# Norm scales from two token columns, spread to rows by transposes

## The reference

```
y = xf * lax.rsqrt(jnp.mean(xf * xf, axis=-1, keepdims=True) + NORM_EPS)
return (y * g.astype(jnp.float32)).astype(x.dtype)
```

```
for l in range(DEPTH):
    h = rms_norm(x, attn_norm_g[l])
    pa, pb, pc = split_sizes(h @ w_in[l], (A_PROJ, B_PROJ, C_PROJ))
    ...
    x = x + jnp.concatenate([ya, yb, yc], axis=-1) @ w_out[l]
    h = rms_norm(x, ffn_norm_g[l])
    x = x + (jax.nn.silu(h @ ffn_w_gate[l]) * (h @ ffn_w_up[l])) @ ffn_w_down[l]
return rms_norm(x, final_norm_g)
```

## Time and profile before

| | |
|---|---|
| Time, median of 3 runs | 939.88 us (939.52 to 940.46) |
| Span of the profiled execution | 938.7 us, with some 1.2 us around it to the median of the runs |
| Instructions in the span | 20423 |
| PE / PEld busy | 916.4 us (98%) / 869.5 us (93%) |
| DVE / ACT busy | 680.7 us (73%) / 555.8 us (59%) |
| Weight chunks on DVE (L277, 256 halves) | 306.0 us, 1224 ns each |
| Weight chunks on ACT (L271, 256 halves) | 259.4 us, 1054 ns each |
| HBM read | 147.26 MB, 158 GB/s over the span |

### The profile page before, as it was taken

How to read it: one execution, slowest core, us unless ns; L and a number is a source line. 1 busy time by engine, 2 the same in 40 slices (tenths; PEclk the granted TensorE clock), 3 DMA queues, 4 the chain that set the end, 5 groups by cost and what they waited for, 6 DMA issues and landing times.

```text
span 938.7 us, 20423 instructions
## 1 busy us (share of the span) xinstructions
PE 916.4 (98%) x8848; PEld 869.5 (93%) x8848; DVE 680.7 (73%) x972; ACT 555.8 (59%) x851; POOL 7.6 (1%) x12
## 2 busy tenths in 40 slices
PE   8899999999999999999999999999999999999996
PEld 7788799999999999878999999999989899989896
DVE  6899667866664589976777666448799679588675
ACT  6873566654443588355754544338587667585665
POOL 0010000000000001000000000000000000000000
PEclk9999999999999999999999999999999999999998
DMA  8342115665554544211466655554544335444231
GB/s 324 151 174 95 48 56 188 214 261 183 201 201 180 180 163 151 98 64 46 140 251 232 250 192 182 204 197 135 179 136 138 132 135 180 147 168 157 93 135 67
DMA packets 24169, 150.94 MB, mean 161 GB/s; under 512 B 2960, under 2 KB 3472, under 8 KB 7056
## 3 DMA queue, kind: packets, MB, share of 16 engines
q1 hardware_dynamic: 24080, 149.64, 44.7%
HBM read 147.26 MB, written 1.05 MB: 158 GB/s over the span
## 4 chain that ended last, share of the span: by engine, by line
PE 67%; DVE 20%; ACT 7%; issue 3%; SPq 1%; DMA 1%; DVEq 0%; ACTq 0%
PE bank L1914 9%; PE bank L1912 8%; PE bank L1913 8%; DVE w_lo L277 6%; PE bank L2145 4%; PE bank L1936 3%; PE bank L1934 3%; PE bank L1935 3%; PE bank L2146 3%; PE bank L2147 3%; ACT w_hi L271 2%; PE bank L1075 1%; PE bank L2177 1%; PE bank L589 1%; PE bank L1165 1%
## 5 line engine op out<-in xcount | busy, mean ns | idle before, releaser
L277 DVE TENSOR_TENSOR w_lo<-w_raw,w_hi 128x1024 fp32r<-128x1024 f32 x256 | 306.0, 1224 | 106.2 <-ACT w_hi L271 105.5
L271 ACT ACTIVATE w_hi<-w_raw 128x1024 fp32r<-128x1024 f32 x256 | 259.4, 1054 | 206.3 <-PE bank L1914 104.9
L1912 PE MATMUL bank<-act_hi,w_hi 128*128 128x256 f32 x704 | 194.5, 276 | 0.0
L1913 PE MATMUL bank<-act_lo,w_hi 128*128 128x256 f32 x704 | 194.3, 276 | 0.0
L1914 PE MATMUL bank<-act_hi,w_lo 128*128 128x256 f32 x704 | 194.3, 276 | 0.0
L1912 PEld LDWEIGHTS bank<-act_hi,w_hi 128*128 128x128 f32 x704 | 132.2, 188 | 0.1
L1913 PEld LDWEIGHTS bank<-act_lo,w_hi 128*128 128x128 f32 x704 | 132.2, 188 | 0.0
L1914 PEld LDWEIGHTS bank<-act_hi,w_lo 128*128 128x128 f32 x704 | 132.2, 188 | 0.0
L2145 PE MATMUL bank<-act_hi,w_hi 128*128 128x256 f32 x352 | 100.2, 285 | 0.3
L2147 PE MATMUL bank<-act_hi,w_lo 128*128 128x256 f32 x352 | 97.7, 278 | 0.0
L2146 PE MATMUL bank<-act_lo,w_hi 128*128 128x256 f32 x352 | 97.7, 278 | 0.0
(11 more groups left out here) (367 smaller groups left out, 1982.1 us busy)
## 6 DMA issues: line engine op xcount, KB each, us to landing
w_raw<-in_w_ffn SPq DMA_DIRECT2D x66, 1024.0 KB, 4.8
w_raw<-in_w_mix SPq DMA_DIRECT2D x62, 1024.0 KB, 4.9
small_w<-in_small SPq DMA_DIRECT2D x2, 1280.0 KB, 7.6
w_raw<-in_w_mix SPq DMA_DIRECT2D x8, 256.0 KB, 6.3
x_res<-in_x_channels SPq DMA_DIRECT2D x4, 256.0 KB, 6.1
probs<-in_w_mix SPq DMA_DIRECT2D x2, 512.0 KB, 7.5
probsT<-in_w_mix SPq DMA_DIRECT2D x1, 1024.0 KB, 10.1
mem<-in_mem_channels SPq DMA_DIRECT2D x1, 1024.0 KB, 7.2
```

The costliest lines, as they stand in the source:

```text
L271: self.nc.scalar.activation(hi, self.piece(self.raw_slot(g), p), ACT.Copy).then_inc(self.hi_ready, 1)
L277: self.nc.vector.tensor_tensor(lo, self.piece(self.raw_slot(g), p), hi.bitcast(fp32), ALU.subtract).then_inc(self.lo_ready, 1)
L1912: TE.matmul(o, hi[:, w], HI[:, k, :], start=(k == 0 and x == 0), stop=False)
L1913: TE.matmul(o, hi[:, w], LO[:, k, :], start=False, stop=False)
```

## The change

`spread` and `scaled_spread` lose the wide matmul and give only the two columns of sums. Root, reciprocal and, in `FoldedNorm`, the products are taken on two columns. A new step, `row_turn`, makes the row: two PE transposes of a column, broadcast over 128 columns, against the identity, put the scale of 256 tokens on every partition in PSUM, and ACT copies the row to `norm_rs` (`row`). The transposes stand inside a chunk: after its first quarter in the mixers (after the second in the stage of `FoldedNorm`, where a second pair turns the first scale), and after the fourth chunk of the feed-forward. The feed-forward's first `gate_sb` moves into the next chunk's halves on DVE, and in the mixers one or two halves of weights move ahead of the first `evacuate`. `settle` is gone. The memory's scale is turned in the same way, without the diagonal. The identity gets a transfer of its own (64 KB), ahead of the small weights.

```
+            last = self.nc.tensor.matmul(bank[:, T + t:T + t + 1], total[:, t * P:(t + 1) * P], ones[:, 0:1],
+                                         start=True, stop=True)
-        self.nc.tensor.matmul(bank[:, 0:T], ones, total, start=True, stop=True).then_inc(self.K.sem("rms_sum"), 1)
+        last.then_inc(self.K.sem("rms_sum"), 1)
...
-        self.nc.scalar.activation(self.K.RSALL[:, :], bank[:, 0:T + NT], ACT.Sqrt, scale=1.0 / D,
+        self.nc.scalar.activation(self.K.RS, bank[:, T:T + NT], ACT.Sqrt, scale=1.0 / D,
...
-        self.nc.vector.reciprocal(self.K.RSALL[:, :], self.K.RSALL[:, :]).then_inc(self.K.sem("rs"), 1)
-        self.wait_rs(dve)
+        self.nc.vector.reciprocal(self.K.RS, self.K.RS).then_inc(self.K.sem("rs"), 1)
+
+    def turn_columns(self, columns, bank):
+
+        for t in range(NT):
+            last = self.nc.tensor.transpose(bank[:, t * P:(t + 1) * P], columns[:, t:t + 1].to_broadcast([P, P]),
+                                            self.K.cst("ident"))
+        return last
+
+    def row_turn(self, pe, bank):
+        pe.wait_ge(self.K.sem("ident_in"), 16)
+        self.wait_rs(pe)
+        self.turn_columns(self.K.RS, bank).then_inc(self.K.sem("rms_sum"), 1)
+
+    def row(self, act, bank):
+        act.wait_ge(self.K.sem("rms_sum"), 2 * self.n + 2)
+        self.nc.scalar.activation(self.K.RSB, bank[:, 0:T], ACT.Copy).then_inc(self.K.sem("rms"), 1)
...
+    def wait_row(self, eng):
+        eng.wait_ge(self.K.sem("rms"), 2 * self.n + 2)
...
-        self.nc.vector.reciprocal(self.R1[:, :], self.K.RSALL[:, :]).then_inc(self.K.sem("first_rs"), 1)
+        self.nc.vector.reciprocal(self.R1[:, T:T + NT], self.K.RS).then_inc(self.K.sem("first_rs"), 1)
...
-            proj(pe, 2)
+            proj(pe, 2, (0,))
+            norm.row_turn(pe, banks[0])
+            proj(pe, 2, (1, 2, 3))
...
-            proj(pe, 1)
+            proj(pe, 1, (0,))
+            norm.row_turn(pe, banks[0])
+            proj(pe, 1, (1, 2, 3))
...
             if i == 2:
                 norm.spread(pe, banks[0])
-                settle(pe)
-        norm.wait_rs(pe)
+            elif i == 3:
+                norm.row_turn(pe, banks[0])
+        norm.wait_row(pe)
...
-        pe.wait_ge(*at("mem_rs_diag", NT))
-        TE.matmul(banks[0][:, 0:T], cst("ones"), DG, start=True,
-                  stop=True).then_inc(*up("inner_sums"))
+        pe.wait_ge(*at("mem_inverse", 1))
+        norm.turn_columns(MRC, banks[0]).then_inc(*up("inner_sums"))
...
-        proj(pe, 2)
+            proj(pe, 2, (0, 1))
+            norm.row_turn(pe, banks[0])
+            norm.first_row_turn(pe, banks[1])
+            proj(pe, 2, (2, 3))
```

More of the change, by code:

```diff
@@ L464, in scaled_spread @@
         for t in range(NT):
-            self.nc.tensor.matmul(bank[:, T + t:T + t + 1], total[:, t * P:(t + 1) * P], ones[:, 0:1], start=True, stop=True)
-        self.nc.tensor.matmul(bank[:, 0:T], ones, total, start=True, stop=True).then_inc(self.K.sem("scaled_rms_sum"), 1)
+            last = self.nc.tensor.matmul(bank[:, T + t:T + t + 1], total[:, t * P:(t + 1) * P], ones[:, 0:1],
+                                         start=True, stop=True)
+        last.then_inc(self.K.sem("scaled_rms_sum"), 1)
@@ L491, in second_inverse, with first_row_turn, first_row, wait_first_row @@
-        self.wait_rs(dve)
+        self.nc.vector.tensor_tensor(RS, RS, self.R1[:, T:T + NT], ALU.mult).then_inc(self.K.sem("rs"), 1)
+    def first_row_turn(self, pe, bank):
+        self.turn_columns(self.R1[:, T:T + NT], bank).then_inc(self.K.sem("scaled_rms_sum"), 1)
+    def first_row(self, act, bank):
+        act.wait_ge(self.K.sem("scaled_rms_sum"), 2)
+        self.nc.scalar.activation(self.R1[:, 0:T], bank[:, 0:T], ACT.Copy).then_inc(self.K.sem("second_rms"), 1)
+    def wait_first_row(self, eng):
+        eng.wait_ge(self.K.sem("second_rms"), 2)
@@ L1651, in _ @@
             st.split_hi(act, 2, 1)
+            norm.row(act, banks[0])
         else:
@@ L1757, in _ @@
             st.split_lo(dve, 2, 1)
+            norm.wait_row(dve)
             evacuate(dve, 0)
@@ L2008, in _ @@
             st.split_hi(act, i + 1, 0)
+            if i == 4:
+                norm.row(act, banks[0])
             st.split_hi(act, i + 1, 1)
@@ L2051, in _ @@
             st.split_lo(dve, i + 1, 0)
+            if i == 4:
+                norm.wait_row(dve)
+                gate_sb(dve, 0)
             st.split_lo(dve, i + 1, 1)
@@ L2331, in turn @@
         if i == 0:
-            norm.wait_rs(pe)
+            norm.wait_row(pe)
+        if i == 1 and layer == 0:
+            norm.wait_first_row(pe)
         TE.matmul(banks[i][:, :], cst("rotb"), PJ[:, S_MBQ + 2 * i:S_MBQ + 2 * i + 2, :],
@@ L2410, in mem_lo, with mem_inverse @@
                                    ALU.mult, ALU.subtract).then_inc(*up("mem_h_lo"))
-    def mem_diagonal(dve, ch):
+    def mem_inverse(dve, ch):
         dve.wait_ge(*at("inner_rms", 1))
[L2414 to L2417, removed]
+        ch(V.reciprocal(MRC[:, :], MRC[:, :]), "mem_inverse")
     def mem_row(dve, ch):
@@ L2442, in _ @@
         norm.spread(pe, banks[0])
-        proj(pe, 1)
         if layer == 0:
+            proj(pe, 1)
             norm.scaled_spread(pe, banks[1])
-        proj(pe, 2)
+            proj(pe, 2, (0, 1))
+            norm.row_turn(pe, banks[0])
+            norm.first_row_turn(pe, banks[1])
+            proj(pe, 2, (2, 3))
+        else:
+            proj(pe, 1, (0,))
+            norm.row_turn(pe, banks[0])
+            proj(pe, 1, (1, 2, 3))
+            proj(pe, 2)
         proj(pe, 3)
@@ L2520, in _ @@
             st.split_hi(act, 3, 1)
+            norm.row(act, banks[0])
+            norm.first_row(act, banks[1])
         else:
```

49 lines of the change are left out of this document (24 added, 25 removed).

## The result

| | us, median (range) | profiled span | PE busy |
|---|---|---|---|
| before | 939.88 (939.52 to 940.46) | 938.7 | 916.4, 98% |
| after | 950.15 (949.36 to 950.75) | 948.8 | 925.2, 98% |

A forecast was written before the change was run, and what follows sets the result against it. PE, busy 98%, was taken as the bound, with waits around the norms. Terms -1.0 - 0.35 + 0.1 - 1.0 - 0.4 = -2.65 us took 939.88 to 937.3 us; range 936.2 to 938.9, eight times in ten 936.1 to 943.9.

The forecast's parts named there:

- Feed-forwards, two of them. PE alone counts.: Both feed-forwards: narrow sums and two transposes cost PE 0.82 us against 1.00 before, -0.18 us each, -0.35 together.
- Rival (a): Feed-forwards fall to the slow pace behind the two transposes: both slow 950.2 us, one 943.7 us; chance 0.19.
- The first mixer of layer 0: First evacuation at 23.3 us instead of 24.32, PE's idle time at the tanh near 1.3 us instead of 2.24; -1.0 us.
- the first mixer of layer 1: PE stalls 0.3 us for the reciprocal before the transposes, DVE's gain ends waiting for PE; +0.1 us (-0.3 to +0.3).
- The second mixers: Layer 0: earlier low half and PE restart, faster pace, cheaper memory scale, -1.0 us; layer 1: mainly faster pace, -0.4 us.
- the paces hoped for: Second mixers: matmuls behind the transposes run fast instead of slow, -0.4 us in layer 0 and -0.65 in layer 1.
- Rival (b): Mixers: the evacuations weren't what PE waited for, so only PE's arithmetic and part of the pace remain; 939.2 us; chance 0.08.
- rival (c): Turned columns: transposes of a broadcast column take 0.27 us each instead of 109 ns, 16 add 2.6 us; 939.9 us; chance 0.03.

The follow-up runs named there:

- e1: Kernel before without the one unread transpose (`settle`) behind the wide matmul of the feed-forwards' sums; 952.85 us, 1.0129 of before.
- e7: Kernel after with before's unread wide matmul and transpose behind the feed-forwards' narrow sums, plus an unread 256-wide reciprocal behind each of seven narrow ones; 939.98 us.
- e9: Kernel after with unread transposes 48 matmuls behind the feed-forwards' turned columns, one in layer 0, two in layer 1; median 938.38 us (937.8 to 945.08).
- e5: Kernel after with the feed-forwards' whole norm as in the kernel before, the change kept in the four mixers alone; 938.07 us, 0.9972 of before.
- e2: Kernel after with one unread transpose (`settle`) put back behind the narrow sums of both feed-forwards; 937.69 us, 0.9971 of before.
- e8: Kernel after with the same list of 32 unread PE interruptions in both layers' feed-forward projections, read by the pace behind each; 973.62 us, one run.

## Why the prediction was wrong

**The step that failed** is "Feed-forwards, two of them. PE alone counts.", the term of -0.18 us for each: it measured +6.06 us. It priced the narrow sums and the turn by their own time and took the 1488 matmuls behind at their old pace. The three instructions that the change drops behind the sums, the wide matmul's two passes and the unread transpose, were put into the sum with their duration ("the unread transpose (0.1 us) is in it"); what they did to the run behind, 6.6 us a layer (1488 times 4.45 ns, of which 1440 fall into the feed-forward and 48 into the next stage), wasn't. The transpose alone is enough for it, as e1 shows. Their own price was right and small: the detours, 162.46 to 163.02 us less one distance, 0.45 us, and 168.56 to 168.90 us less one, 0.22, make 0.67 us against 1.00 before, -0.33 instead of -0.18. With 1440 times 4.45 ns, 6.4 us, that gives the +6.06 us.

**Rival (a)** had the size of the loss and the stages right (950.2 us against 950.15) and its cause wrong, so that it came so near is in part luck: it blamed the transposes of the turn, which here came 48 matmuls after the loss. It got 0.11 because the evidence was read for the wrong instruction. What could have been seen in the trace of before: of its five wide sums without `settle` four stood ahead of matmuls at 117.8 ns (one of them at 333.87 us) and only one, at 647.32 us, ahead of 113.3 ns. With `settle`, in both feed-forwards, they stood ahead of 113.3 ns. I saw that the transpose stood there and asked what two transposes would do in its place, not what its loss would do to the sums.

**The other steps.** The first mixer of layer 0 went nearly as forecast. Its chain of waits after (start us, us, what), beside the earlier trace rows:

```profile
22.72 0.23 PE bank L427 x2
...
22.97 0.40 ACT norm_rs L438
...
23.39 0.70 DVE proj L1354
```

The evacuation starts at 23.39 us (forecast 23.3, before 24.32). PE's wait at the tanh fell to 1.75 us, not to 1.3:

```profile
28.79 0.45 PE L824 MATMUL bank<-rwkv_bufs,small_w 64*128 64x256 f32 x1 [1.75 <-ACT rwkv_bufs L1215]
```

That instruction comes 0.84 us earlier, though PE's first projection started 0.47 us later than before, and the stage ends 1.07 us ahead: term -1.0. In the first mixer of layer 1 the 0.3 us stall before the turn didn't come: DVE's reciprocal was through at 339.9, PE reached the turn at 340.24 us. DVE's second evacuation waits for PE there as forecast, and the stage cost 0.35 us more instead of 0.1, just outside of the stated -0.3 to +0.3. Of this 0.21 us is the feed-forward's slow pace carried over: the 47 distances ahead of this stage's sums take 5.53 us, 5.32 before.

```profile
339.74 0.17 DVE L422 RECIPROCAL norm_rs<-norm_rs 128x2 f32<-128x2 f32 x1
...
344.90 0.69 DVE L1354 TENSOR_TENSOR proj<-bank,norm_rs 128x512 f32<-128x512 f32 x1 [1.65 <-PE bank L1170]
```

The second mixers gave 0.74 and 0.55 us against 1.0 and 0.4. The low half that PE resumed on stands at 664.04 us; less the 11.39 us by which after is behind when the stage begins that is 652.65, against 654.05 before and 653.1 forecast. Two of the paces hoped for there came (113.3 ns, once the first distances are past, behind the turns at 669.02 and 804.62 us). Rival (b) fails by e7 (DVE's time was what PE waited for in the first mixer and in the second of layer 0), rival (c) too: the turned columns' matmuls took 270 to 294 ns each, and two of them held PE 0.22 us in all.

The Trainium skill, page "TensorE: Matmul & The Clock Gate", section "Back-to-back issue gap", says that in a stream of weight loads and matmuls the spacing is set by both operations, and gives one distance per width. The runs don't contradict the first half, the slow pace having one longer weight load in three (192 ns against 188), but these 4 ns aren't the 13 that three distances gain, so they don't show it either. They don't agree with the second: the same 128x256 stream has two distances, 113.3 and 117.8 ns, at a granted clock of 1.00.

**Left open:** what in PE makes the two paces, why one order of instructions ends in one pace and another in the other, and why one transpose in a slow stretch comes out either way from execution to execution. No run tells that. So the cause is shown as far as the instruction whose loss slows the feed-forwards, and not how it does so. Nor is it shown that it has to be a transpose: the wide matmul alone doesn't do it (0 fast, 5 slow), and no other instruction was put in its place.

## What to carry to other kernels

Before an unread or tiny instruction on a saturated engine is removed or moved, count what runs uninterrupted behind it and compare the distance of the instructions there in both traces: 4.5 ns on 2976 matmuls outweighed every wait that this change removed. The place to look is the first point at which the two traces' distances differ, which may lie well ahead of the new instructions. And repeat the timing: a placement such as e9's looks cured in six runs of ten. Of the versions run here, the change in the mixers with the feed-forwards' sums kept as they were (e5, 938.07 us) or with `settle` put back behind the narrow sums (e2, 937.69 us) beats the kernel before by 0.3% and the changed one by over 1%, and the two can't be told apart.

## What the runs showed of the hardware

- A stream of 128x256 matmuls with a weight load each ran at 113.3 or at 117.8 ns, at a granted clock of 1.00 in both, and kept its pace for up to 1488 matmuls, until the next interruption. In the slow pace every third weight load took 192 ns instead of 188, and which of three it was differed from stretch to stretch.
- In the feed-forwards the pace behind an interruption depended on the interruption and on the pace ahead of it: narrow sums behind a fast stretch 28 of 28 slow, with the wide matmul and a transpose 15 of 15 fast. In the stage of `FoldedNorm` narrow sums behind a fast stretch were 9 of 9 fast.
- Most places repeated (32 of 32 between two layers of e8); with one transpose in a slow stretch of one layer and two in the other it didn't, with times 6 us apart in the same kernel.
- Transposes of a broadcast column cost PE no more than plain ones: two held it 0.22 us with the way back.
